# Feed-forward activations of a two-block transformer turned by VectorE and a trip through DRAM

## The chip, the core and the metric

One core of one Trainium2 chip runs the kernel. The metric is the device time of one launch in microseconds (us), the median of the timed runs. The engines are named as in the profile: PE is TensorE (PEld its weight loads), DVE is VectorE, ACT is ScalarE, POOL is GpSimd, SP is SyncE, which here only issues DMAs.

## What is computed

Two transformer blocks on a sequence of 256 tokens with 1024 features, all in f32. Cut to what matters, with the attention and mixing parts named only:

```python
# first block
h = rmsnorm(x, attn_norm_g);  qa, ka, va, qb, kb, vb = split(h @ w_in)
out_a = attention(rope(rmsnorm(qa)), rope(rmsnorm(ka)), va)      # 8 query heads, 2 key heads
out_b = differential_attention(rmsnorm(qb), rmsnorm(kb), vb, lam, rel_bias)
x = x + concat(out_a, out_b) @ w_out
u = square(relu(rmsnorm(x, mlp_norm_g) @ w_up))                  # 256 x 4096
x = x + u @ w_down
# second block; sh, sc, g come from silu(c) @ w_ada + b_ada
u = rms_norm(x, ffn1_norm_g) * (1 + sc1) + sh1
a, b = split(u @ ffn1_w_in);  x = x + 0.5 * g1 * ((silu(a) * b) @ ffn1_w_out)   # 256 x 2816
x = x + g2 * mixing(x)                                           # mLSTM, forgetting attention, gates
a, b = split(u3 @ ffn2_w_in); x = x + 0.5 * g3 * ((silu(a) * b) @ ffn2_w_out)   # 256 x 2816
```

## The kernel before, in words

Every product with weights is made of three TensorE matmuls on fp32r halves. A weight or activation W is split into an upper part hi (its value rounded to fp32r) and a lower part lo = W - hi, and A @ W is taken as Ahi@Whi + Ahi@Wlo + Alo@Whi (lines 1217, 1221 and 1222, in the function `half`). The moving operand is 512 columns of weights, the stationary one 128x128 of the activation, turned so that features lie on partitions. There are two tiles t of 128 tokens. So each 128x512 piece of weights costs 6 matmuls, 3 for each tile.

Weights come in units of two such pieces (128 x 1024 numbers, 512 KB). A unit goes through three steps. SP issues its DMA into one of four `raw` buffers, ACT writes `whi` (L1525), and DVE writes `wlo` (L1907). There are five pairs of `whi` and `wlo` (NW = 5), and three lent ones at the start of a stage. SP may issue the load of a unit when DVE is done with the unit four before it, and ACT may make `whi` when PE is done with the unit five before it.

The order of all work is made ahead by a planner (`plan`). It walks over the halves (a unit on one tile), and after each half it ticks a list of jobs. The table LAG says how many ticks a job waits between its steps, LO says how many halves DVE's `wlo` stands behind ACT's `whi` in each stage, and ADA says after how many halves a step of the modulation is made. Such a step multiplies 512 KB of w_ada (an `araw` buffer, line 2247) by silu(c) on DVE. Each engine then works through its own list strictly in order, and semaphores connect them. PACED names the blocks with several ticks for each half.

In a feed-forward stage PE makes a block of 512 hidden columns (`up0` to `up7`, or `a` and `b` of a gated one). For `up` ACT takes relu from PSUM into a buffer `nat` and DVE squares it (L2292). For a gated block DVE multiplies the two (L2302). The result has tokens on partitions and must be turned for the next product. The job has two steps (`turn_segments`), each with 4 TensorE transposes of 128x128 against `ident` (L1270, 256 hidden columns of both tiles) into a bank of PSUM. ACT copies the bank to the upper part (`uh`, L1627), and DVE writes the lower part from the bank and the upper part (`ul`, L1911). The first block has 8 hidden blocks of 512. Each of ffn1 and ffn2 has 5 of 512 and one of 256 columns. That makes 16 + 11 + 11 = 38 banks, so 152 transposes.

In the attention stage the blocks of w_in come in the order qb, kb, vb, qa, ka. A plain head (qa, ka) is normed and rotated by tables (rope, a chain of DVE operations, lines 2036 to 2098). qb and kb are only normed. The scores of the differential part start when qb and kb are there, and those of the plain part when qa and ka are.

Of the kernel before, what the change touches and what calls it, by code (L numbers as in the profile page):

```python
# [21 lines left out]
LAG = {("attn", "sums"): 5, ("attn_a", "wait"): 21, ("attn_as", "round"): 4, ("attn_as", "wait"): 0,  # L22
       ("attn_as", 0): 6, ("attn_as", 1): 4, ("attn_as", 2): 3, ("attn_as", 3): 12, ("attn_at", "round"): 8,
       ("attn_at", 0): 4, ("attn_at", 1): 5, ("attn_at", 2): 3, ("attn_at", 3): 3, ("attn_at", 4): 1,
       ("attn_at", 5): 10, ("attn_at", 6): 1, ("attn_at", 7): 17, ("attn_aw", "round"): 3, ("attn_aw", 0): 4,
       ("attn_aw", 1): 3, ("attn_aw", 2): 8, ("attn_aw", 3): 1, ("attn_aw", 4): 7, ("attn_aw", 5): 4,
       ("attn_aw", 6): 1, ("attn_aw", 7): 17, ("attn_b", "wait"): 2, ("attn_bm", "round"): 10, ("attn_bm", 0): 2,
       ("attn_bm", 1): 1, ("attn_bm", 2): 2, ("attn_bm", 3): 4, ("attn_bs", "round"): 4, ("attn_bs", "wait"): 0,
       ("attn_bs", 0): 4, ("attn_bs", 1): 4, ("attn_bs", 2): 4, ("attn_bs", 3): 4, ("attn_bt", "round"): 5,
       ("attn_bt", 0): 1, ("attn_bt", 1): 6, ("attn_bt", 2): 7, ("attn_bt", 3): 1, ("attn_bw", "round"): 16,  # L30
       ("attn_bw", 0): 2, ("attn_bw", 1): 2, ("attn_bw", 2): 3, ("attn_bw", 3): 1, ("conv", 0): 3, ("conv", 1): 3,
       ("conv", 2): 4, ("end", "late"): 3, ("end", "lead"): 4, ("ffn1", "between0"): 0, ("ffn1", "between1"): 0,
# [2783 lines left out]
```

## Time and profile before

| what | us |
|---|---|
| median of 3 timed runs | 980.27 (980.14 to 983.6) |
| the profiled execution, its own time | 980.24 |
| its span, first to last instruction | 978.9 |
| PE busy in it | 963.1 (98%) |
| DVE, ACT, POOL busy | 701.4, 523.0, 56.2 |

The span leaves out 1.3 us of the execution. A busy PE here is not PE at its peak, since each matmul's recorded duration overlaps the next one's. What a matmul takes from the path is the distance from its start to the next start. The share of a stage that an engine is busy is read from the view by stretches, and what ended an idle stretch from the view of waits.

### The profile page before, as it was taken

To read this page: it belongs to the slowest core of one execution; us is meant where nothing else is said; L and a number is where in the kernel's file an instruction comes from. 1 tells how busy PE (TensorE), PEld (TensorE's weight loads), DVE (VectorE), ACT (ScalarE), POOL (GpSimd) and SP (SyncE) were. 2 spreads that over 40 slices of the span, in tenths; PEclk is the share of its full clock that TensorE was granted. 3 is DMA by queue.
4 is the path that set the end of the run, shared out by engine and by line. 5 is a ranking of instruction groups with operands and counts; after the bars stand their busy time and mean duration, and the time that the engine had idled before them with its cause. 6 is when DMAs were issued, how large, how long until landed. Compare 5 with 4: busy or idle time off the path is not lost.

```text
span 978.9 us, 12466 instructions
## 1 busy us (share of the span) xinstructions
PE 963.1 (98%) x4614; PEld 792.9 (81%) x4614; DVE 701.4 (72%) x1045; ACT 523.0 (53%) x800; POOL 56.2 (6%) x62
## 2 busy tenths in 40 slices
PE   9988999999999999999999999999999999999998
PEld 7777888888888888888788888877888878888886
DVE  6787678987776676687669987578768764555553
ACT  7576665554446444443576565477554474444431
POOL 2311000000000000000000121121000000000000
PEclk9999999999999999999999999999999999999999
DMA  9641768887894888888747775865637535555561
GB/s 342 216 151 44 237 214 279 299 292 258 291 359 137 297 275 276 280 276 291 250 128 228 246 238 175 269 214 187 213 119 245 195 118 184 171 185 193 203 215 43
DMA packets 110122, 216.19 MB, mean 221 GB/s; under 512 B 8242, under 2 KB 15562, under 8 KB 109806
## 3 DMA queue, kind: packets, MB, share of 16 engines
q1 hardware_dynamic: 109918, 215.13, 65.5%
q8 instruction: 36, 0.59, 0.2%
q10 hardware_dynamic: 144, 0.27, 0.1%
q14 instruction: 24, 0.20, 0.1%
HBM read 214.29 MB, written 2.13 MB: 221 GB/s over the span
## 4 chain that ended last, share of the span: by engine, by line
PE 91%; DVE 3%; ACT 2%; DMA 2%; issue 1%; POOL 0%; SPq 0%; ACTq 0%; DVEq 0%; POOLq 0%
PE ps L1217 28%; PE ps L1222 27%; PE ps L1221 27%; PE ps L1270 3%; PE ps L1357 2%; PE ps L1312 1%; PE ps L1338 1%; DMA NF<-scr_g 1%; PE ps L1248 1%; ACT whi L1525 1%; DMA raw<-in_w_mix 1%; DVE wlo L1907 1%; DMA raw<-in_w_in 0%; DVE nat L1990 0%; DVE x L1994 0%
## 5 line engine op out<-in xcount | busy, mean ns | idle before, releaser
L1525 ACT ACTIVATE whi<-raw 128x1024 fp32r<-128x1024 f32 (+1 forms) x300 | 311.4, 1047 | 263.0 <-PE ps L1222 208.0
L1907 DVE TENSOR_TENSOR wlo<-raw,whi 128x1024 fp32r<-128x1024 f32 (+1 forms) x300 | 358.1, 1211 | 70.9 <-ACT whi L1525 70.3
L1217 PE MATMUL ps<-whi,hTh 128*128 128x512 f32 (+1 forms) x800 | 319.7, 400 | 1.1 <-ACT hTh L1537 1.1
L1221 PE MATMUL ps<-wlo,hTh 128*128 128x512 f32 (+1 forms) x800 | 311.1, 389 | 0.0
L1222 PE MATMUL ps<-whi,hTl 128*128 128x512 f32 (+1 forms) x800 | 311.0, 389 | 0.0
L1217 PEld LDWEIGHTS ps<-whi,hTh 128*128 128x128 f32 x800 | 150.8, 189 | 32.3 <-issue 2.2
L1222 PEld LDWEIGHTS ps<-whi,hTl 128*128 128x128 f32 x800 | 150.7, 188 | 32.0
L1221 PEld LDWEIGHTS ps<-wlo,hTh 128*128 128x128 f32 x800 | 150.9, 189 | 28.6 <-issue 0.4
L2502 POOL TENSOR_TENSOR stat<-stat,mhalf 128x8 f32<-128x8 f32 (+3 forms) x29 | 36.2, 1259 | 606.0 <-DVE stat L1923 485.8
L1217 PE MATMUL ps<-whi,uh_ffn 128*128 128x512 f32 x176 | 69.2, 393 | 0.0
L1222 PE MATMUL ps<-whi,ul_ffn 128*128 128x512 f32 x176 | 68.6, 390 | 0.0
L1221 PE MATMUL ps<-wlo,uh_ffn 128*128 128x512 f32 x176 | 68.6, 390 | 0.0
L1911 DVE TENSOR_TENSOR ul_ffn<-ps,uh_ffn 128x512 fp32r<-128x512 f32 x22 | 15.2, 691 | 70.5 <-ACT uh_ffn L1627 70.5
L2247 DVE CUSTOM_DVE_ANT_0 araw<-araw,crow,colp 128x1024 f32<-128x1024 f32 x48 | 61.3, 1278 | 0.8 <-DMA araw<-in_w_mod 0.6
L1217 PE MATMUL ps<-whi,uh 128*128 128x512 f32 x128 | 50.3, 393 | 0.0
L1222 PE MATMUL ps<-whi,ul 128*128 128x512 f32 x128 | 49.9, 390 | 0.0
L1221 PE MATMUL ps<-wlo,uh 128*128 128x512 f32 x128 | 49.9, 389 | 0.0
L1222 PEld LDWEIGHTS ps<-whi,ul_ffn 128*128 128x128 f32 x176 | 33.0, 188 | 7.0
L1221 PEld LDWEIGHTS ps<-wlo,uh_ffn 128*128 128x128 f32 x176 | 33.1, 188 | 6.7
L1217 PEld LDWEIGHTS ps<-whi,uh_ffn 128*128 128x128 f32 x176 | 33.1, 188 | 6.7
L2263 DVE SCALAR_TENSOR_TENSOR gate<-araw,cs,gate 128x512 f32<-128x512 f32 x42 | 32.4, 771 | 1.6 <-DMA araw<-in_w_ada 0.8
L1270 PE MATMUL ps<-ident,nat 128*128 128x128 f32 x208 | 31.1, 272 | 2.5 <-DVE nat L2089 1.4
(256 smaller groups left out, 1074.3 us busy)
## 6 DMA issues: line engine op xcount, KB each, us to landing
raw<-in_ffn_w_in SPq DMA_DIRECT2D x80, 512.0 KB, 4.6
raw<-in_w_mix SPq DMA_DIRECT2D x64, 512.0 KB, 4.5
araw<-in_w_mod SPq DMA_DIRECT2D x48, 512.0 KB, 5.3
raw<-in_ffn_w_out SPq DMA_DIRECT2D x44, 512.0 KB, 4.2
raw<-in_w_up SPq DMA_DIRECT2D x32, 512.0 KB, 5.2
raw<-in_w_down SPq DMA_DIRECT2D x32, 512.0 KB, 5.6
araw<-in_w_ada SPq DMA_DIRECT2D x24, 512.0 KB, 4.9
raw<-in_w_out SPq DMA_DIRECT2D x16, 512.0 KB, 3.8
```

The lines of the kernel that those rows point to most:

```text
L1217: pe.e.matmul(o, ah, h[:, j, :], start=s0, stop=False, skip_group_check=True)
L1221: pe.e.matmul(o, ah, l[:, j, :], start=False, stop=False, skip_group_check=True)
L1222: r = pe.e.matmul(o, al, h[:, j, :], start=False, stop=s1, skip_group_check=True)
L1248: r = pe.e.transpose(bank[:, c * 128:(c + 1) * 128], src[:, (4 * p + c) * 128:(4 * p + c + 1) * 128], ident[:, :])
L1270: r = pe.e.transpose(bank[:, c * 256 + t * 128:c * 256 + t * 128 + 128], src[t][:, (2 * p + c) * 128:(2 * p + c + 1) * 128], ident[:, :])
L1357: r = pe.e.matmul(ob[:, h * 64:(h + 1) * 64], buf[:, (nk * c + k) * 128:(nk * c + k + 1) * 128], (fV if a["fox"] else VA)[:, k, v0:v0 + 64 ...
L1525: act.e.activation(uflat(whi, u), uflat(raw, u), ACT.Copy).then_inc(hi.up(u), 1)
L1907: v.tensor_tensor(uflat(wlo, u), uflat(raw, u), uflat(whi, u).bitcast(f32), SUB).then_inc(lo_dve.up(u), 1)
L1911: v.tensor_tensor(o, bank, h.bitcast(f32), SUB).then_inc(lower.up(name, p), 1)
L2247: v.tensor_tensor_reduce(out=w, in0=w, in1=crow[:, :], scale=1.0, scalar=col("bada", 8 * m + i), op0=MUL, op1=ADD, accum_out=modc[:, 8 * m ...
L2263: r = v.scalar_tensor_tensor(acc, buf[:, k, :], cs[:, kt:kt + 1], acc, MUL, ADD)
L2502: g.tensor_tensor(o, a, mhalf[:, 0:n], ALU.pow).then_inc(rstd.up(*key), 1)
```

## The change

It has four parts.

1. The turned activation of each feed-forward block no longer goes over TensorE. DVE transposes the 128x512 `nat` tile in blocks of 32x32 into a `sq` buffer (`swaps`). SP stores that to DRAM (`scr_u`, 256 KB) and reads it back in another order of rows, as runs of 512 bytes, into one of four new landing buffers (`land_m`, `land_f`; `shuttle`). ACT copies it to `uh` (`uppers_of`) and GpSimd makes `ul` from both (`lowers_of`). The order of features that results is not the natural one, so the rows of w_down, ffn1_w_out and ffn2_w_out are permuted on the host, ahead of the launch.
2. qa is the first block of the attention stage, ahead of qb, kb, vb, ka.
3. PE's wait for an activation of these stages is now on GpSimd's lower part, for each tile.
4. All numbers of LAG, LO and ADA are new. ADA for the mlp stage goes from 3 to 4 and for y from 4 to 7, LO for mlp from 3 to 1, and for u_mlp from 3 to 0.

```diff
-       ("gates", 3): 11, ("gates", 4): 1, ("glu", "turn"): 5, ("glu", 0): 8, ("heads", "turn"): 5, ("heads", 0): 5,
+       ("gates", 3): 12, ("gates", 4): 2, ("glu", "fetch"): 3, ("glu", "upper"): 5, ("glu", "lower"): 4,
...
-PACED = ("kb", "vb", "qa", "ka", "ob0", "ob1", "gb0", "gb1")
-ADA = {"attn": 0, "ffn1": 4, "ffn2": 7, "merged": 8, "mix": 11, "mixT": 0, "mlp": 3, "u_ffn1": 4, "u_ffn2": 6,
-       "u_mlp": 3, "y": 4, "yb": 5}
-LO = {"attn": 3, "begin": 5, "ffn1": 3, "ffn2": 3, "merged": 0, "mix": 3, "mixT": 3, "mlp": 3, "u_ffn1": 1,
-      "u_ffn2": 0, "u_mlp": 3, "y": 2, "yb": 0}
+PACED = ("qb", "kb", "vb", "qa", "ka", "ob0", "ob1", "gb0", "gb1")
+ADA = {"attn": 0, "ffn1": 4, "ffn2": 8, "merged": 8, "mix": 11, "mixT": 0, "mlp": 4, "u_ffn1": 4, "u_ffn2": 5,
+       "u_mlp": 3, "y": 7, "yb": 5}
+LO = {"attn": 3, "begin": 2, "ffn1": 3, "ffn2": 0, "merged": 0, "mix": 3, "mixT": 3, "mlp": 1, "u_ffn1": 0,
+      "u_ffn2": 4, "u_mlp": 0, "y": 0, "yb": 2}
...
-    for key, c0, n in (("qb", 768, 512), ("kb", 1280, 512), ("vb", 1792, 512), ("qa", 0, 512), ("ka", 512, 256)):
-        block(key, "w_in", 0, 8, c0, n, "attn", small=6 * (key == "qb"))
+    for key, c0, n in (("qa", 0, 512), ("qb", 768, 512), ("kb", 1280, 512), ("vb", 1792, 512), ("ka", 512, 256)):
+        block(key, "w_in", 0, 8, c0, n, "attn", small=6 * (key == "qa"))
...
+        def shuttle(name, kind):
+            land = land_of(name)
+            for t in range(2):
+                while None not in sqr.held or None not in land.held:
+                    yield 1
+                sqr.take(name, t)
+                land.take(name, t)
+            seg(name)
+            natural_end(name)
...
+            yield lag(kind, "fetch", 3)
+            seg(name)
+            yield lag(kind, "upper", 3)
+            seg(name)
+            yield lag(kind, "lower", 1)
+            seg(name)
...
-            yield from turn_segments(name, 2, "u")
-            natural_end(name)
+            yield from shuttle(name, "u")
...
         if act[:2] == "u_":
-            return lower(f"{act[2:]}g{k // 4}", p)
+            return u_low(hidden(act, k), t)
...
+        def uppers_of(name, dst, c0, n):
+            for t in range(2):
+                act.wait_ge(*ld_u[land_of(name).at(name, t)](name, t))
+                act.e.activation(by_blocks(dst, c0, n, t), landed(name, t, n), ACT.Copy).then_inc(upper.up(name, t), 1)
...
+        def swaps(name, ready, n):
+            for t in range(2):
+                dve.wait_ge(*ready(name, t))
+                dve.wait_ge(*sqr.free(name, t))
+                v.transpose(sqr.buf(name, t)[:, 0:n], nat.buf(name, t)[:, 0:n]).then_inc(swapped.up(name, t), 1)
+                nat.give(swapped(name, t), name, t)
...
+        def lowers_of(name, h, l, c0, n):
...
+            for t in range(2):
+                pool.wait_ge(*upper(name, t))
+                g.tensor_tensor(by_blocks(l, c0, n, t), landed(name, t, n), by_blocks(h, c0, n, t).bitcast(f32),
+                                SUB).then_inc(u_low.up(name, t), 1)
+                land_of(name).give(u_low(name, t), name, t)
...
+            for t in range(2):
+                sp.wait_ge(*swapped(name, t))
+                sp.wait_ge(*land.free(name, t))
+                i = sqr.at(name, t)
+                q.dma_start(bass.AP(scrU.tensor, land.at(name, t) * 65536, [[n, 128], [1, n]]),
+                            sqr.buf(name, t)[:, 0:n]).then_inc(st_u[i].up(name, t), 16)
+                sqr.give(st_u[i](name, t), name, t)
+            yield
+            for t in range(2):
+                sp.wait_ge(*st_u[sqr.at(name, t)](name, t))
+                sp.wait_ge(*mm(*behind))
+                q.dma_start(land.buf(name, t)[:, 0:n].rearrange("p (a x) -> p a x", a=4),
+                            bass.AP(scrU.tensor, land.at(name, t) * 65536, [[n // 4, 128], [32 * n, 4], [1, n // 4]])).then_inc(
+                                ld_u[land.at(name, t)].up(name, t), 16)
```

DVE in the middle of the `up` stage, one block of 512 hidden columns. L2247 and L2288 are the modulation step, L2292 and L2340 the square. Before:

```order
208 L2292 TENSOR_TENSOR nat<-nat 128x512 x2
209 L1911 TENSOR_TENSOR ul<-ps,uh 128x512
210 L1907 TENSOR_TENSOR wlo<-raw,whi 128x1024
211 L2247 ISA araw,modc<-araw,crow,colp 128x1024
212 L2247 ISA modc 128x1
213 L1911 TENSOR_TENSOR ul<-ps,uh 128x512
214 L1907 TENSOR_TENSOR wlo<-raw,whi 128x1024
215 L2247 ISA araw,modc<-araw,crow,colp 128x1024
216 L2247 ISA modc 128x1
217 L1907 TENSOR_TENSOR wlo<-raw,whi 128x1024 x2
```

And now:

```order
214 L2340 TENSOR_TENSOR nat<-nat 128x512 x2
215 L1948 TENSOR_TENSOR wlo<-raw,whi 128x1024
216 L2288 ISA araw,modc<-araw,crow,colp 128x1024
217 L2288 ISA modc 128x1
218 L1948 TENSOR_TENSOR wlo<-raw,whi 128x1024
219 L2333 STREAM_TRANSPOSE sq<-nat 128x512 x2
220 L1948 TENSOR_TENSOR wlo<-raw,whi 128x1024
221 L2288 ISA araw,modc<-araw,crow,colp 128x1024
222 L2288 ISA modc 128x1
223 L1948 TENSOR_TENSOR wlo<-raw,whi 128x1024
```

Two transposes of SBUF stand where two lower parts from PSUM stood, and a block has 2 modulation steps where it had 2 or 3.

SP in the same stage; `araw` is a modulation load. Before:

```order
40 L2611 DMA raw<-in_w_up 128x2x512 x2
41 L2654 DMA araw<-in_w_mod 128x1024
42 L2611 DMA raw<-in_w_up 128x2x512
43 L2654 DMA araw<-in_w_mod 128x1024
44 L2611 DMA raw<-in_w_up 128x2x512 x2
```

And now, one block:

```order
47 L2682 DMA raw<-in_w_up 128x2x512
48 L2705 DMA scr_u<-sq 128x512 x2
49 L2682 DMA raw<-in_w_up 128x2x512
50 L2745 DMA araw<-in_w_mod 128x1024
51 L2712 DMA land_m<-scr_u 128x4x128 x2
52 L2682 DMA raw<-in_w_up 128x2x512 x2
53 L2745 DMA araw<-in_w_mod 128x1024
```

Two stores, each behind a wait for DVE's transpose, and two loads, each behind a wait for its store, stand among 4 weight loads and 2 modulation loads.

PE at the end of block ka, from its last weight matmul on. `kd` holds the rotated keys, VB and PT belong to the differential part, `over` and PA to its softmax. Before:

```order
252 L1222 MATMUL ps<-whi,hTl 128x256
253 L1270 MATMUL ps<-ident,nat 128x128 x4
254 L1372 MATMUL ps<-VB,PT 128x128 x4
255 L1338 MATMUL ps<-ident,over 128x128 x4
256 L1270 MATMUL ps<-ident,nat 128x128 x4
257 L1372 MATMUL ps<-VB,PT 128x128 x8
258 L1270 MATMUL ps<-ident,kd 128x128 x4
259 L1312 MATMUL ps<-kaT,qaT 128x256 x8
260 L1338 MATMUL ps<-ident,P 128x128 x8
```

And now:

```order
250 L1266 MATMUL ps<-whi,hTl 128x256
251 L1356 MATMUL ps<-kbT,qbT 128x256 x4
252 L1382 MATMUL ps<-ident,PA 128x128 x4
253 L1416 MATMUL ps<-VB,PT 128x128 x4
254 L1382 MATMUL ps<-ident,over 128x128 x4
255 L1416 MATMUL ps<-VB,PT 128x128 x4
256 L1314 MATMUL ps<-ident,kd 128x128 x4
257 L1382 MATMUL ps<-ident,over 128x128 x4
258 L1356 MATMUL ps<-kaT,qaT 128x256 x8
259 L1416 MATMUL ps<-VB,PT 128x128 x4
```

The transposes of the queries are gone from here, one group of four scores of the differential part has come in, and 8 of the products with VB now stand behind the plain scores.

## Rows read from the trace of the kernel before

**Rows 1.** The page, busy time and instructions of each engine:
```profile
PE 963.1 (98%) x4614; PEld 792.9 (81%) x4614; DVE 701.4 (72%) x1045; ACT 523.0 (53%) x800; POOL 56.2 (6%) x62
```
**Rows 2.** The page, chain that ended last, shares of the span by engine:
```profile
PE 91%; DVE 3%; ACT 2%; DMA 2%; issue 1%; POOL 0%; SPq 0%; ACTq 0%; DVEq 0%; POOLq 0%
```
**Rows 3.** PE's waits: who it waited for, us in total, times, longest:
```profile
PE ps L1270 <- DVE nat L2089: 1.4, 1, 1.4
...
PE ps L1270 <- DVE kd L2098: 1.2, 1, 1.2
```
**Rows 4.** Time line of PE: start us, us, engine, line, operation:
```profile
143.30 0.39 PE L1217 MATMUL ps<-whi,hTh 128*128 128x512 f32 x1
...
143.76 0.39 PE L1222 MATMUL ps<-whi,hTl 128*128 128x512 f32 x1
143.99 0.60 PE L1270 MATMUL ps<-ident,nat 128*128 128x128 f32 x4
144.34 0.48 PE L1217 MATMUL ps<-whi,hTh 128*128 128x512 f32 x1
144.66 0.40 PE L1221 MATMUL ps<-wlo,hTh 128*128 128x512 f32 x1
```
**Rows 5.** Time line of DVE in the up stage:
```profile
194.44 0.68 DVE L1911 TENSOR_TENSOR ul<-ps,uh 128x512 fp32r<-128x512 f32 x1
195.04 1.21 DVE L1907 TENSOR_TENSOR wlo<-raw,whi 128x1024 fp32r<-128x1024 f32 x1
196.17 1.27 DVE L2247 CUSTOM_DVE_ANT_0 araw<-araw,crow,colp 128x1024 f32<-128x1024 f32 x1
197.38 0.08 DVE L2247 DVE_READ_ACCUMULATOR2_ANT modc<- 128x1 f32 x1
```
**Rows 6.** Stretches: us, PE, PEld, DVE, ACT, POOL busy, PEclk, DMA share, GB/s:
```profile
190.00:201.00 11.00, 11.00 (x54) 9.12 (x53) 10.27 (x14) 6.37 (x8) 0.00 (x0) 1.00 0.91 308
...
267.00:278.00 11.00, 11.00 (x50) 9.13 (x49) 8.70 (x11) 4.25 (x4) 0.00 (x0) 1.00 1.01 390
...
396.00:418.00 22.00, 22.00 (x102) 18.21 (x101) 15.74 (x19) 10.56 (x12) 0.00 (x0) 1.00 0.85 283
```
**Rows 7.** DVE groups, shapes apart: busy us, mean ns:
```profile
L2292 DVE TENSOR_TENSOR nat<-nat 128x512 f32<-128x512 f32 x16 | 10.9, 689 | 6.3 <-ACT nat L1756 6.2
...
L1947 DVE CAST hTh<-sq 128x512 fp32r<-128x512 f32 x8 | 3.4, 424 | 2.1 <-ACT sq L1563 1.9
```
**Rows 8.** Time line of POOL and DVE in the mixing stage:
```profile
643.57 2.53 POOL L2538 TENSOR_TENSOR nat<-nat,row 128x512 f32<-128x512 f32 x2 [5.13 <-ACT nat L1839]
...
644.92 2.27 DVE L1907 TENSOR_TENSOR wlo<-raw,whi 128x1024 fp32r<-128x1024 f32 x1 [2.60 <-ACT whi L1525]
```
**Rows 9.** Time line of ACT and PE, one weight unit (whi at 187.50, PE at 199.30):
```profile
187.50 1.06 ACT L1525 ACTIVATE whi<-raw 128x1024 fp32r<-128x1024 f32 x1 [1.66 <-PE ps L1222]
...
199.30 0.39 PE L1221 MATMUL ps<-wlo,hTh 128*128 128x512 f32 x1
```
**Rows 10.** DMA issues: queue, operation, KB each, median us to landing:
```profile
raw<-in_w_up SPq DMA_DIRECT2D x32, 512.0 KB, 5.2
...
biasT<-scr_b SPq DMA_DIRECT2D x8, 128.0 KB, 2.5
out<-x SPq DMA_DIRECT2D x4, 256.0 KB, 2.2
```
**Rows 11.** SP's waits, the longest on a store: us in total, times, longest:
```profile
SPq L2639 <- DMA scr_b<-scr_t: 5.1, 1, 5.1
```
**Rows 12.** Time line of PE and DVE at the end of block ka:
```profile
67.96 0.28 PE L1222 MATMUL ps<-whi,hTl 128*128 128x256 f32 x1
...
77.74 3.16 PE L1312 MATMUL ps<-kaT,qaT 64*128 64x256 f32 x16 [0.78 <-ACT kaT L1605]
...
72.57 0.27 DVE L2036 TENSOR_REDUCE stat<-sq 128x2 f32<-128x128 f32 x1
...
75.35 0.89 DVE L2098 TENSOR_TENSOR kd<-nat,stat 128x128 f32<-128x128 f32 x4
```

More of the change, by code:

```diff
@@ L19 @@
 NEVER = (None, 0)
[L22 to L32, printed above, removed]
@@ L263, in build @@
     sX.close()
+    sY = ExitStack()
+    sb("under_mlp", [128, 16384], c=sY)
+    land_m = Ring([sb(f"land_m{i}", [128, 512], c=sY) for i in range(4)])
+    sY.close()
+    sZ = ExitStack()
+    sb("under_ffn", [128, 14336], c=sZ)
+    land_f = Ring([sb(f"land_f{i}", [128, 512], c=sZ) for i in range(4)])
+    sZ.close()
     whi += [lent_hi[j] for j in range(LENT)]
@@ L282, in build, with land_of @@
     scrG = nc.dram_tensor("scr_g", (24, 256), f32, kind="Internal").ap()
+    scrU = nc.dram_tensor("scr_u", (4, 128, 512), f32, kind="Internal").ap()
+    def land_of(name):
+        return land_m if name[:2] == "up" else land_f
     columns = {}
@@ L495, in half @@
             at["act"] = blocks[units[u][0]]["act"]
+            if at["act"][:2] == "u_":
+                drain_of([hidden(at["act"], k) for k in range(units[u][2], units[u][2] + units[u][3])])
             for w in lows:
@@ L798, in plan @@
         at["ada"] = ada()
[L799 removed]
+        pairs.take("qa")
         for k in range(8):
@@ L807, in plan @@
             order.append(("first_lo", k))
-        first = blocks["qb"]["units"]
+        first = blocks["qa"]["units"]
         for u in first:
@@ L868, in job_glu @@
             yield lag("glu", 0, 3)
-            yield from turn_segments(name, (n + 255) // 256, "glu")
-            natural_end(name)
+            yield from shuttle(name, "glu")
         def ffn(m, last_gate, stage, then=None):
@@ L2293, in up_job @@
             yield
-            yield from lowers(name, 2, uh["mlp"], ul["mlp"], 4 * c)
+            swaps(name, squared, 512)
+            yield
+            yield
+            yield
         def glu_job(m, i, n):
@@ L2304, in glu_job @@
             yield
-            yield from lowers(name, n // 256, uh[m], ul[m], 4 * i)
+            swaps(name, glu, n)
+            yield
+            yield
+            yield
         def gates_job():
@@ L2625, in row, with shuttle @@
                 load_row(d["b_mix"], at + c * 512, name)
+        def shuttle(name, n, behind):
+            land = land_of(name)
+            yield
+            for t in range(2):
+                sp.wait_ge(*swapped(name, t))
[4 more added lines that the diff above has]
+                sqr.give(st_u[i](name, t), name, t)
+            yield
+            for t in range(2):
+                sp.wait_ge(*st_u[sqr.at(name, t)](name, t))
[3 more added lines that the diff above has]
+                                ld_u[land.at(name, t)].up(name, t), 16)
+            yield
+            yield
         def bias_job():
@@ L2712, in sync_program @@
         jobs = {"bias": bias_job(), "ada": ada(), "gates": gates_job()}
+        for c in range(8):
+            jobs[f"up{c}"] = shuttle(f"up{c}", 512, (blocks["up0"]["units"][LENT - 1], 1))
+        for m, last in (("ffn1", "down1"), ("ffn2", "wob1")):
+            for i in range(6):
+                jobs[f"{m}g{i}"] = shuttle(f"{m}g{i}", 512 if i < 5 else 256, last_half(last))
         for what, *of in order:
@@ L2804, with shuttled @@
     w_mod = np.stack([np.asarray(inputs["w_ada_2"])[0, :, m * D:(m + 1) * D].T for m in (0, 1, 3, 4, 6, 7)])
+    def shuttled(name):
+        w, n = data[name][0], data[name].shape[1]
+        full = w[:n // 512 * 512].reshape(-1, 4, 4, 32, w.shape[1]).transpose(0, 2, 3, 1, 4).reshape(-1, w.shape[1])
+        rest = w[n // 512 * 512:].reshape(-1, 4, n % 512 // 128, 32, w.shape[1]).transpose(0, 2, 3, 1, 4) if n % 512 else w[:0]
+        return np.ascontiguousarray(np.concatenate([full, rest.reshape(-1, w.shape[1])])[None])
+    data.update({name: shuttled(name) for name in ("w_down", "ffn1_w_out", "ffn2_w_out")})
     data.update(w_mod=np.ascontiguousarray(w_mod), colp=np.ascontiguousarray(colp), w_gate=w_gate,
```

89 lines of the change are left out of this document (57 added, 32 removed), and 25 rows, old and new, of the table LAG.

## The prediction, made before the changed kernel was run

> **What bounds the kernel now.** I read the page first. PE is busy 98% of the span [rows 1], and the chain that ended last lies on PE for 91% of it, with DVE, ACT and DMA at 2 or 3% each [rows 2]. So the kernel is bound by the number and pitch of TensorE instructions. PE's waits, read next, are short and few. The long ones of the attention stage are 1.4 and 1.2 us [rows 3], and in the time line of starts I count 6.4 us of such gaps between 67.9 and 82 us. In the up stage and the gated ones PE waits for nothing: it is busy 11.00 of 11.00 us in each stretch [rows 6].
>
> Whatever leaves PE's list in those stages therefore shortens the run by its whole pitch, as long as the other engines keep up. The stretches say which could fail to. In the up stage DVE is busy 10.27 of 11 us and the DMA engines have a share of 0.91 [rows 6]. In the gated stage DVE has 15.74 of 22 and DMA 0.85.
>
> **What a group of four transposes costs.** Weight matmuls start 0.23 us apart: two of them take 143.30 to 143.76 [rows 4]. Around a group the start of the matmul ahead is 143.76 and the second start behind it 144.66, which is 0.90. Two pitches of that are 0.45, so a group of four costs 0.45. It is more than the 0.35 from 143.99 to 144.34, since the first matmul behind it takes 0.32 and not 0.23. There are 38 such groups, all in stages where PE never waits, and the other 37 have the same spacing within 0.02. **Term 1: 38 x 0.45 = -17.1 us.**
>
> **What takes their place.** For each hidden block (8 in the first stage, 6 in each gated one, 20 in all) and each tile there are now a DVE transpose, a store, a load, an ACT copy and a GpSimd subtraction, so 40 of each (4 of them half as wide). PE sees them only if an activation or a weight is late.
>
> *The activations themselves.* up7 ends before down0 starts and is read by its last eighth, 28 halves of 1.37 us = 38 us later. Its steps are 5 + 1 + 15 + 2 ticks, at one tick a half, 31 us, and the order holds the last within it. The last gated block needs 1 + 3 + 5 + 4 ticks and is read at the last two of 22 halves. Cost 0, hidden behind the product with the blocks ahead. If a trip took 7 us longer than its ticks, this cover would be gone and the excess would be paid once in each of three stages.
>
> *ACT.* 40 copies replace 38 from PSUM of the same size. ACT is busy 6.4 of 11 us, so cost 0.
>
> *DVE.* The transpose is not in the trace. Its bounds are a 128x512 cast at 0.42 us and a 128x512 product at 0.69 us [rows 7]. I take 0.69 less the overlap, 0.61, the start-to-start of the lower part that it replaces (194.44 to 195.04 [rows 5]), because that row is limited to one element at a time as well. The Trainium skill, "Vector Engine (DVE) Microarchitecture Reference", § 3.8, says the 32x32 transpose sustains one element per cycle per lane, so a row of a tile would take what the product takes; no run here shows it, and the sum would be the same.
>
> One block of the up stage takes PE 48 x 0.227 = 10.9 us. DVE has in it, by starts: 4 wlo x 1.13 (195.04 to 196.17), 2 modulation steps x 1.21, 2 squares x 0.69 and 2 transposes x 0.61 [rows 5, 7] = 9.5 us, against 10.3 before. That alone is a little relief.
>
> *GpSimd against DVE.* The 128x512 product of GpSimd takes 1.3 us (two in 2.53), and while the second of them ran, from about 644.8 to 646.1, DVE's wlo of 644.92 took 2.27 us and not 1.21 [rows 8, 5]. So a GpSimd operation that reads two SBUF tiles holds back a DVE operation that does. The Trainium skill, "SBUF — State Buffer", § Who interferes with whom, states this as an exclusive lock on a port pair, held for a whole instruction, between GpSimd reads and a DVE instruction with two SBUF inputs; by that rule, the trace agrees, with 1.06 us lost in one meeting. Nearly all DVE work of a block (wlo, modulation, square) is of that kind. Two subtractions a block cost DVE between 0 (they fall beside a transpose or an idle moment) and 2 x 1.3 = 2.6 us, and I take 2.2 since DVE is seldom idle. DVE then needs 9.5 + 2.2 = 11.7, in the worst case 12.1, of 10.9 us. Over 8 blocks it falls 6 to 10 us behind. The strided 32-element runs that GpSimd now reads are not in the trace. I take the contiguous price and keep a dearer one for a rival.
>
> *DMA.* A block moves 4 weights and 2 modulation loads of 0.524 MB and 4 shuttle transfers of 0.262 MB: 4.19 MB in 10.9 us is 385 GB/s, against 308 at a share of 0.91 before. The highest stretch before is 390 GB/s at a share of 1.01, and 308 at 0.91 would give 338 at a full share [rows 6]. So the engines are full: a block takes 10.7 to 12.4 us of them, a lag of 0 to 1.5 a block over about 7 blocks, 0 to 10 us. I take the row of 390, since a saturated queue is the state ahead, so under 1 us in all.
>
> *The slack.* A unit's whi starts at 187.50, as PE lets go of the buffer, its wlo ends at 194.5 and PE reads it at 199.30 [rows 9, 5]: 4.8 us to spare. LO for this stage goes from 3 to 1 halves, which gives up to 2 x 1.37 = 2.7 more, so 7.5. DVE's and DMA's lags run side by side and draw on the same slack. DVE's 6 to 10 less 7.5 leaves 0 to 3. **Term 2: +3 us** in the up stage and the start of down, with ends 0 (the lags stay inside the slack) and 12 (10 of DMA and 10 of DVE in part one after the other, less 7.5).
>
> *SP.* Its list is in order, so a store waits for DVE's transpose and a load for its store, and weight loads queue behind both. A store of 256 KB lands in 2.2 us, and the one wait on a store through DRAM was 5.1 us [rows 10, 11]. One weight and one modulation load stand between store and load in the up stage, so SP is held some 2 to 4 us once a block. The weight behind it is late by as much, inside the same 7.5 us. The load itself resembles the 128 KB read of biasT from DRAM (2.5 us) up to the 5.2 of a weight.
>
> *The gated stages.* A block of 512 columns takes PE 21.8 us. DVE had 15.74 of 22, and 2.6 more fit. DMA goes from 283 GB/s to 283 + 48 = 331 [rows 6], inside 338 to 390. **Term 3: +0.5 us**, ends 0 and 3.
>
> **Attention.** The plain queries' rotation now comes in the first blocks, where PE has other weights. Before, PE ended ka at 67.96 and began the plain scores at 77.74, 9.8 us later. DVE did two weights and the rest of the queries' rotation first. The keys' chain began at 72.57 and ended with kd at 76.24, 3.7 us [rows 12]. Now DVE has four masked softmax steps of about 0.5 us ahead of it, which wait for scores about 0.6 us behind the block's end. So kd is there after 0.6 + 2.0 + 3.7 = 6.3 us. What is late next is the last pair of softmax parts (1.3 us more), whose transposes stand ahead of the plain scores. They start about 8.0 us after the block and not 9.8, with about as many PE instructions in between. 8 products with VB now fill the wait for the first exponentials. The differential part has less weight work to hide behind (vb and ka, not vb, qa and ka), which can bring new gaps of a like size. **Term 4: -1.5 us**, ends -3.5 and +4.
>
> **The other numbers** of LAG move steps in the mixing stage, where no PE work is added or removed and PE's gaps sum to under 6 us. I take 0, ends -2 and +2.
>
> **The sum.** 978.9 - 17.1 + 3 + 0.5 - 1.5 = 963.8 us of span. The execution is 1.3 longer: 965.1. The profiled execution (980.24) and the median (980.27) are the same, so nothing is corrected. Predicted: 965 us, a ratio of 0.984.
>
> **Rivals.**
> 1. *The up stage runs at DVE's or the DMA engines' pace.* For it: DVE's 11.7 to 12.1 of 10.9 us and 385 GB/s asked for. Against it: 7.5 us of slack, and less load as soon as `down` begins. Term 2 is then 8 to 12, so 970 to 974.
> 2. *GpSimd's strided subtraction is dear, and the run is slower than before.* For it: no row has its pattern, and DVE is held for as long as it runs. Against it: the contiguous row of 1.3 us. With a price p, a block needs 9.5 + 2p of DVE, and 8 blocks lose 8 x (9.5 + 2p - 10.9) - 7.5. From p = 2.5 the loss exceeds the 18 us gained; at 3.3 it is 34 us, and 965 - 3 + 34 = 996. It decides in the up stage, where PE would wait on wlo.
> 3. *The lags stay inside the slack and attention closes its gaps.* Term 2 is 0 and term 4 is -3.5: 978.9 - 17.1 - 3.5 + 1.3 = 959.6, say 960 to 962.
> 4. *The gain is given back in pieces*, late activations after each stage, SP held behind stores, and new gaps in attention: +6, +3 and +4 on top of term 2, so about 977.
>
> **Chances.** The forecast (962 to 969) 0.53, rival 3 0.12, rival 1 0.2, rival 4 0.08, rival 2 0.07. A measurement of this kernel can tell about 0.5% (4.9 us) from no change. Faster by more than that means below 975.4: 0.53 + 0.12 + 0.2 + a little of rival 4 = 0.87. Within it: 0.06. Slower: 0.07. The range from 960 to 976 holds the first three and leaves out rival 2, most of rival 4 and the edge of rival 3.
>
> **What would show it.** Term 1: 152 fewer transposes, and PE's starts around the `up` blocks 0.23 us apart throughout. Term 2: in the stretches of the up stage PE's busy time stays near 11.00 of 11, DVE's goes above 10.3, wlo operations of over 2 us appear beside GpSimd's, and the DMA share is near 1. If PE's waits name wlo or whi there for more than 8 us, rival 1 holds. GpSimd's subtraction at about 1.3 us clears rival 2, and above 2.5 it proves it. Term 4: the plain scores begin about 8 us after ka's last matmul. The prediction is wrong if GpSimd's price, the landing of the 512-byte runs (above 7 us) or a clock that falls in the new gaps is other than taken here.

## The result and the profile after

| | changed kernel | before, on the same chip |
|---|---|---|
| median of 5 runs, us | 974.52 (971.50 to 975.37) | 983.41 (980.14 to 986.04) |
| ratio | 0.9915, 95% interval 0.9894 to 0.9937 | 1 |
| profiled span, us | 974.0 | 978.9 |

The change makes the kernel 0.85% faster, where 1.6% was forecast. The time lies in the range and the direction is right, but half of the gain is missing. A few executions, among them one of e6 and one of e7 below, ran at a much lower granted clock (1350 to 1816 us) and are left out of all ratios. The page of the changed kernel, busy time by engine (it answers to [rows 1]) and the chain that ended last by engine ([rows 2]):

```profile
PE 949.5 (97%) x4462; PEld 780.3 (80%) x4462; DVE 719.1 (74%) x1047; ACT 524.6 (54%) x803; POOL 124.9 (13%) x102
```
```profile
PE 80%; DMA 8%; DVE 6%; ACT 3%; issue 2%; POOL 1%; SPq 0%; DVEq 0%; ACTq 0%; POOLq 0%
```

The 152 transposes are gone and PE's busy time fell by 13.6 us, but the span only by 4.9. The chain was on PE for 91% and is now for 80%, with DMA at 8%. To see where, I noted the start of PE's first weight matmul of each stage. The table has the lengths of the stages in the profiled runs, in us. The first stage begins with PE's first weight matmul, 6 us into the span, the last ends with the span, and e2, e7 and e10 come below:

| stage | before | changed | e2 | e7 | e10 |
|---|---|---|---|---|---|
| start to up | 113.7 | 113.0 | 113.0 | 115.1 | 112.5 |
| up | 93.8 | 88.0 | 88.0 | 88.1 | 88.0 |
| down | 91.1 | 102.3 | 90.1 | 90.2 | 94.0 |
| ffn1, both products | 188.4 | 182.5 | 181.7 | 181.8 | 182.3 |
| mixing | 293.1 | 294.2 | 293.7 | 293.5 | 297.4 |
| ffn2, both products | 192.6 | 187.7 | 187.7 | 187.7 | 187.1 |

The up stage gained all that its 12 groups were to give. What is missing was lost in down, which has 4 groups fewer and still takes 11.2 us more. Stretches of the changed kernel, the view of [rows 6], with the same columns. The first one spans the end of up (down starts at 207.3 us), the others lie in down:

```profile
201.00:212.00 11.00, 11.00 (x50) 9.13 (x49) 10.03 (x11) 6.17 (x8) 3.14 (x2) 1.00 1.02 365
212.00:223.00 11.00, 10.81 (x48) 8.63 (x47) 8.17 (x10) 6.32 (x8) 3.51 (x2) 1.00 1.01 339
223.00:234.00 11.00, 10.12 (x42) 7.35 (x40) 10.35 (x10) 5.28 (x6) 3.28 (x3) 1.00 0.93 329
234.00:245.00 11.00, 8.79 (x36) 6.60 (x36) 7.37 (x9) 3.18 (x3) 0.00 (x0) 1.00 1.00 349
245.00:256.00 11.00, 6.03 (x16) 4.78 (x17) 9.26 (x9) 4.63 (x7) 3.17 (x2) 0.69 0.96 324
256.00:267.00 11.00, 11.00 (x50) 9.10 (x49) 7.69 (x10) 5.55 (x9) 0.00 (x0) 1.00 0.79 250
```

DVE is not busy throughout, so it isn't what is late. Its waits and ACT's between 200 and 250 us show who is: `wlo` waits for `whi`, and `whi` for the loads of w_down. The gate row of the modulation (L1450) then waits for DVE, once and long:

```profile
ACT whi L1555 <- DMA raw<-in_w_down: 23.9, 14, 6.8
DVE wlo L1948 <- ACT whi L1555: 7.4, 4, 3.3
...
PE ps L1450 <- DVE gate_lo L2310: 5.4, 1, 5.4
...
PE ps L1261 <- DVE wlo L1948: 2.9, 5, 1.3
```

PE's time line there, and the clock behind it in stretches of 4 us:

```profile
244.18 0.39 PE L1266 MATMUL ps<-whi,ul 128*128 128x512 f32 x1
249.97 0.77 PE L1450 MATMUL ps<-row_hi,ones 128*128 128x512 f32 x1 [5.40 <-DVE gate_lo L2310]
...
250.97 0.63 PE L1261 MATMUL ps<-whi,uh 128*128 128x512 f32 x1
251.39 0.63 PE L1265 MATMUL ps<-wlo,uh 128*128 128x512 f32 x1
```
```profile
248.00:252.00 4.00, 2.03 (x5) 1.68 (x6) 4.00 (x3) 2.24 (x3) 2.96 (x2) 0.56 0.99 274
252.00:256.00 4.00, 4.00 (x13) 3.10 (x12) 2.30 (x4) 0.01 (x1) 0.00 (x0) 0.59 0.88 334
256.00:260.00 4.00, 4.00 (x19) 3.31 (x18) 2.53 (x4) 2.11 (x2) 0.00 (x0) 1.00 0.55 165
```

By starts (what the distance to the next start exceeds the usual 0.227 us by), PE's waits in down add up to 10.5 us, 5.6 of them before the gate row; in e2, which has the same list, 1.0. The granted clock is at its half level (1.2 GHz) from 248.5 to 255.3 us. PE stands idle for the first 1.5 us of that, and from 249.97 on 12 starts follow each other at 0.43 us and more, not 0.23, which costs 2.6 more. Together 9.5 + 2.6 = 12.1 us, of the 12.2 that down takes beyond that of e2 (90.1, where 91.1 - 1.8 = 89.3 would be without the 4 groups): nearly the whole loss.

**Why the loads are late.** The weights' lead over PE (from the end of a unit's `wlo` to PE's first use of it) drains for the most part before down, in up: it is 8.0 to 8.5 us in the middle of up, 1.7 at its end and 0.4 in down. From 150 to 215 us the DMA view of the changed kernel shows (first the GB/s in 40 slices of 1.6 us, then the issues: queue, operation, KB each, median us from issue to landing):

```profile
GB/s 315 268 391 418 391 340 366 269 306 338 412 378 210 253 222 303 353 377 403 421 300 297 320 308 266 359 413 413 287 259 297 333 334 401 408 401 320 346 368 261
DMA packets 13899, 21.82 MB, mean 336 GB/s; under 512 B 826, under 2 KB 5946, under 8 KB 13895
...
raw<-in_w_up SPq DMA_DIRECT2D x14, 512.0 KB, 7.5
...
scr_u<-sq SPq DMA_DIRECT2D x10, 256.0 KB, 9.0
```

The time line of SP's issues, one and a half blocks (L2705 stores, L2712 reads back):

```profile
175.48 0.33 SPq L2745 DMA_DIRECT2D araw<-in_w_mod  x1
181.78 1.02 SPq L2712 DMA_DIRECT2D land_m<-scr_u  x2
182.84 1.02 SPq L2682 DMA_DIRECT2D raw<-in_w_up  x2
183.90 0.47 SPq L2745 DMA_DIRECT2D araw<-in_w_mod  x1
184.41 0.47 SPq L2682 DMA_DIRECT2D raw<-in_w_up  x1
185.08 2.66 SPq L2705 DMA_DIRECT2D scr_u<-sq  x2
187.79 0.68 SPq L2682 DMA_DIRECT2D raw<-in_w_up  x1
188.53 0.56 SPq L2745 DMA_DIRECT2D araw<-in_w_mod  x1
194.33 1.05 SPq L2712 DMA_DIRECT2D land_m<-scr_u  x2
```

SP issues nothing between 175.8 and 181.8 and between 189.1 and 194.3, since the next item in its list must wait for the store, which takes 9 us to land behind the loads already queued. Afterwards SP issues the overdue loads in one burst, behind which the next store waits again. The rate stays high during most of a hold (353 to 421 GB/s in the slices from 176 to 182 us) and falls behind it: 300 to 266 from 182 to 191 us, 287 and 259 from 195.5, and 210 to 253 from 169.5, behind a hold that ended at 169.1. The queue never runs empty, though. By issue and landing at least 3 transfers (1.3 MB) are under way at each microsecond from 150 to 232. So the time line ties the lower rate to the holds, but doesn't show what inside the DMA engines lowers it. The share of 0.99 in this window also fits another reading, that the engines can give no more than 336 GB/s with this mix of runs. So there were four theories:

- **A**: the DMA engines are at their limit, some 340 GB/s.
- **B**: SP, held by the wait for the store, issues weight loads too late.
- **C**: GpSimd's subtractions hold DVE, and DVE is late.
- **D**: the new numbers (LO, the modulation's pace) cost the time, not the trip.

### The profile page after: what moved, and what is told of

It is laid out like the page before. It is cut to its first block, busy times and chain, and to the rows that moved or that the text cites. A ratio compares the mean times of both kernels' runs of the same rounds, so it can differ in the third digit from the quotient of the medians.

```text
span 974.0 us, 12407 instructions
## 1 busy us (share of the span) xinstructions
PE 949.5 (97%) x4462; PEld 780.3 (80%) x4462; DVE 719.1 (74%) x1047; ACT 524.6 (54%) x803; POOL 124.9 (13%) x102
## 4 chain that ended last, share of the span: by engine, by line
PE 80%; DMA 8%; DVE 6%; ACT 3%; issue 2%; POOL 1%; SPq 0%; DVEq 0%; ACTq 0%; POOLq 0%
PE ps L1261 24%; PE ps L1266 24%; PE ps L1265 24%; DMA raw<-in_w_up 3%; DVE wlo L1948 2%; DMA araw<-in_w_ada 2%; PE ps L1401 2%; PE ps L1314 1%; ACT whi L1555 1%; PE ps L1356 1%; DMA raw<-in_w_down 1%; PE ps L1382 1%; DMA NF<-scr_g 1%; DMA scr_u<-sq 1%; PE ps L1292 1%
## 5 line engine op out<-in xcount | busy, mean ns | idle before, releaser
L1948 DVE TENSOR_TENSOR wlo<-raw,whi 128x1024 fp32r<-128x1024 f32 (+1 forms) x300 | 369.2, 1245 | 128.1 <-ACT whi L1555 127.1
L2646 POOL TENSOR_TENSOR ul_ffn<-land_f,uh_ffn 128x512 fp32r<-128x512 f32 (+1 forms) x24 | 40.4, 1703 | 229.5 <-ACT uh_ffn L1798 229.5
L2288 DVE CUSTOM_DVE_ANT_0 araw<-araw,crow,colp 128x1024 f32<-128x1024 f32 x48 | 64.4, 1341 | 0.0
L2646 POOL TENSOR_TENSOR ul<-land_m,uh 128x512 fp32r<-128x512 f32 x16 | 27.0, 1707 | 100.2 <-ACT uh L1798 100.2
```

The costliest lines, as they stand in the source:

```text
L1948: v.tensor_tensor(uflat(wlo, u), uflat(raw, u), uflat(whi, u).bitcast(f32), SUB).then_inc(lo_dve.up(u), 1)
L2288: v.tensor_tensor_reduce(out=w, in0=w, in1=crow[:, :], scale=1.0, scalar=col("bada", 8 * m + i), op0=MUL, op1=ADD, accum_out=modc[:, 8 * m ...
L2646: g.tensor_tensor(by_blocks(l, c0, n, t), landed(name, t, n), by_blocks(h, c0, n, t).bitcast(f32), SUB).then_inc(u_low.up(name, t), 1)
```

## The experiments

Each ratio is to the kernel before on the same chip, from four to six runs.

| run | ratio (95%) | span, us | down, us |
|---|---|---|---|
| e1 thin modulation loads | 0.9779 (0.9757 to 0.9800) | 959.8 | 89.2 |
| e2 fetch after 4 ticks | 0.9786 (0.9762 to 0.9810) | 960.5 | 90.1 |
| e3 up by TensorE | 0.9866 (0.9844 to 0.9887) | 969.8 | 91.9 |
| e4 modulation slower in down | 0.9835 (0.9809 to 0.9862) | 967.7 | 97.9 |
| e5 read back by GpSimd's queue | 0.9801 (0.9782 to 0.9820) | 959.3 | 89.5 |
| e6 fetch after 2 ticks | 0.9916 (0.9888 to 0.9944) | 966.9 | 96.7 |
| e7 e2 with old attention | 0.9837 (0.9814 to 0.9861) | 962.3 | 90.2 |
| e8 e2, lower parts by DVE | 0.9815 (0.9795 to 0.9834) | 962.4 | 90.0 |
| e9 changed kernel again | 0.9914 (0.9890 to 0.9938) | 973.4 | 102.9 |
| e10 e2 with old pace and LO | 0.9851 (0.9833 to 0.9869) | 967.5 | 94.0 |
| e11 fetch after 8 ticks | 0.9794 (0.9774 to 0.9814) | 960.0 | 89.7 |

### Bytes or waits: e1 and e2

e1 cuts the bytes (the modulation loads of up and down bring 32 KB each and not 512, so its modulation isn't the model's):

```diff
+                if 2 <= n < 32:
+                    dst, src = araw.buf(n)[:, 0, 0:64], d["w_mod"][0, 0:128, 0:64]
                 q.dma_start(dst, src).then_inc(ld_ada[araw.at(n)].up(n), 16)
```

> Loads 2 to 31 of the modulation (those of the up and the down stage) move 32 KB and not 524 KB; all waits, the order and DVE's work on the buffers stay. The modulation computed is therefore a wrong one, so the time tells only what the bytes cost. Theory A (the DMA engines are full in the up stage and in the first third of down, at about 340 GB/s where 385 are asked for): the demand falls to about 300 GB/s in up and 200 in down, weights are never late, the down stage takes about 89 us and not 102.4, the whole about 962 us (ratio to the kernel before 0.979). Theory B (SP's in-order list, which waits 37 us for the completion of stores between 150 and 250 us, makes the weight loads late): the waits stand where they stood, at most 3 us gained, 971 to 974. Theory C (GpSimd's subtraction holds DVE and DVE is what is late): no change, 974.

e2 keeps them and moves the wait:

```diff
-       ... ("u", "fetch"): 1, ("u", "upper"): 15,
+       ... ("u", "fetch"): 4, ("u", "upper"): 12,
```

> In the up stage SP reads a block back 4 ticks after its store and not 1, and ACT's copy comes 12 ticks after that and not 15, so bytes and activation times are the same but 3 ticks (4 us) of weight loads now stand between store and load. Theory B (SP's wait for the store is what delays the weights): SP's waits for stores fall from 37 us to under 10, and 5 to 8 us are gained, 967 to 970. Theory A (the DMA engines' capacity): the same bytes in the same stage, 973 to 975.5, no difference. Theory C: no change.

e1 took 961.3 us, as A said, and e2 961.8, better than B said. Alone, e1 would have shown the wrong cause. B was wrong to expect that the waits stay when the bytes go: a store behind shorter queues lands sooner, and SP's waits for stores (150 to 250 us) fell from 37.4 us to 11.4. e2 decides, since it moves the same bytes. The same DMA view, 150 to 215 us, of e2:

```profile
GB/s 275 347 410 417 373 329 383 367 398 421 406 370 384 412 408 403 401 399 366 403 393 401 377 396 381 366 383 386 371 381 371 374 379 417 405 384 406 397 358 402
DMA packets 16289, 25.02 MB, mean 385 GB/s; under 512 B 953, under 2 KB 7097, under 8 KB 16285
...
raw<-in_w_up SPq DMA_DIRECT2D x14, 512.0 KB, 6.3
...
scr_u<-sq SPq DMA_DIRECT2D x10, 256.0 KB, 5.6
```

The deep dips are gone (the rate stays above 325 after the first slice), the mean is 385 and not 336 GB/s, and a store lands in 5.6 us. The stretch from 150 to 215 us by engine, of the changed kernel and then of e2, with the share of the DMA engines and the rate at its end:

```profile
150.00:215.00 65.00, 65.00 (x288) 53.86 (x287) 54.46 (x64) 33.38 (x42) 17.05 (x10) 1.00 0.99 336
```
```profile
150.00:215.00 65.00, 65.00 (x289) 53.81 (x288) 61.03 (x71) 39.35 (x48) 19.11 (x12) 1.00 1.05 385
```

The waits of SP's queue in that window, of the changed kernel and then of e2, show what took their place, the wait for DVE to free a buffer, which the table of `raw` buffers makes in any case:

```profile
SPq L2712 <- DMA scr_u<-sq: 26.8, 10, 6.0
...
SPq L2682 <- DVE wlo L1948: 2.7, 6, 0.7
```
```profile
SPq L2682 <- DVE wlo L1948: 17.1, 21, 1.8
...
SPq L2712 <- DMA scr_u<-sq: 8.3, 12, 2.1
```

PE waits for nothing between 112 and 270 us, and the slow clock in down is gone with the gap ahead of it. A falls. B's 5 to 8 us was too small, because it counted late weights alone and neither the gate row nor the clock behind it.

### The same wait on another engine: e5

In the blocks of the up stage SP's list has neither the wait nor the load, and GpSimd's has both at the same step:

```diff
+                    pool.wait_ge(*st_u[sqr.at(name, t)](name, t))
+                    pool.wait_ge(*mm(blocks["up0"]["units"][LENT - 1], 1))
+                    g.dma_start(land.buf(name, t)[:, 0:512]...
```

> As the changed kernel, with its fetch lag of 1 and all its numbers, but the 16 loads that bring a block of the up stage back are issued by GpSimd's queue, and GpSimd waits there for the store, not SP. The bytes, the issue order of all other loads and the moment from which a block may be read back stay. Theory B (SP, held in its in-order list by the wait for a store, issues the weight loads late and the DMA queues run empty): with the wait gone from SP's list the gain of the late fetch comes fully, 960 to 963 us, and the stretches of the up stage show about 385 GB/s. Theory A (the DMA engines give no more than some 340 GB/s with this mix of short and long runs): 973 to 976.

961.3 us, and the mean from 150 to 215 us is 381 GB/s. The fetch is as early as in the changed kernel and no lag moved. But one thing more differs. The DMA view of e5 for 150 to 215 us has hardly a packet of 512 bytes:

```profile
DMA packets 10814, 24.76 MB, mean 381 GB/s; under 512 B 940, under 2 KB 940, under 8 KB 10810
```

Issued by GpSimd, the read-back went in packets of 4096 bytes and not of 512, so e5 alone could also speak for a dear read in short runs. e2 excludes that, since it keeps these packets (7097 under 2 KB) and reaches 385 GB/s. Taken together, the wait's place in SP's list is the cause, and not the read itself. The Trainium skill, "DMA: Bandwidth & Descriptors", § Issuing engines are not separate DMA queues, says that issuing from several engines saves only the issuing sequencer's time, usually small beside the transfer. That it saves nothing more agrees with these runs, as e2, with one issuing engine, reaches the same rate (385). What the sequencer lost here was not small, as it held a wait.

### The dose: e6 and e11

The diff is that of e2, with 2 and 14, and with 8 and 8.

> A dose between the changed kernel (fetch after 1 tick, 974.5) and e2_late_fetch (4 ticks, 961.8): 2 ticks of 1.37 us, ACT's copy one tick less behind it. Theory B: the hold for each store falls by about 1.4 us from 5.7 to some 4, and as the backlog in the queue sets the rest, the gain is partly there: 964 to 970, with SP's waits for stores between 150 and 250 us at 20 to 30 us in sum. Had the late fetch helped by some other effect of the shifted steps (a threshold at the copy's time), 2 ticks would read as 1, 974, or as 4, 962, with SP's wait not in proportion.

> The changed kernel with the fetch after 8 ticks and the copy 8 ticks behind it (1 and 15 there, 4 and 12 in e2). Theory B says that all is gained once the store has landed before SP comes to it: SP's waits for stores go from 9.9 us in sum to 0 and there is nothing left to gain, 960.5 to 962. If SP's list mattered through the place of the load and not through the wait, 8 would go on from 4, below 959, or turn back.

e11 took 962.1 us with no wait for a store at all in SP's list between 150 and 250 us: four ticks were enough, as B says. e6 missed its mark. Its waits for stores came to 30.5 us there (37.4 in the changed kernel), and its ratio is that of the changed kernel. Its runs spread from 968.3 to 975.4, and the profiled one is the fastest, so its 96.7 us of down flatter it. The gain doesn't follow the dose, and 2 ticks read as 1, which the expectation had given to the other theory, a threshold somewhere in the shifted steps. e5 speaks against that, as it moved no step and gained all. A likely reason is that a tick (1.37 us) counts only once SP comes so late that no burst builds up, whose loads make the next store late; that wasn't tried by itself.

### The numbers or the trip: e3, e4, e10

e3 sends up0 to up7 over TensorE again (turn, copy and lower part as in the kernel before, rows of w_down in natural order):

```diff
+            if int(name[2]) in BY_PE:
+                yield 10
+                yield from turn_segments(name, 2, "u")
+                natural_end(name)
+                return
             yield lag("u", 0, 4)
             yield from shuttle(name, "u")
```

> Only the up stage goes back to TensorE's transposes: its 8 blocks have 16 groups of 4 transposes, ACT and DVE make the parts from PSUM, and the rows of w_down are in natural order. The gated stages and every number of the tables stay as in the changed kernel. The transposes cost 16 x 0.45 = 7.2 us. Theory A: the demand in up falls from 385 to about 290 GB/s and the 13 us lost in down and its slow clock come back: 974.5 + 7.2 - 13 = 969. Theory D (the 13 us come from the new table numbers, LO 1 and 0 and the modulation's pace, and not from the trip through DRAM): 974.5 + 7.2 = 982.

969.5 us: up back at 93.8, down at 91.9, as theory A had forecast. B, which then has no store to wait for, says the same. D falls. In the up stage the trip as built was a loss of 5 us, and all of the change's gain came from the gated stages. With the late fetch it gains 8 there.

e4 changes two numbers of ADA:

```diff
-ADA = {"attn": 0, "ffn1": 4, ...
+ADA = {"attn": 0, "ffn1": 3, ...
...
-       "u_mlp": 3, "y": 7, "yb": 5}
+       "u_mlp": 4, "y": 7, "yb": 5}
```

> The modulation's pace in the down stage is one step each 4 halves and not 3, and in ffn1 3 and not 4, so 4 of its loads (2.1 MB) move from down to ffn1. Theory A: the demand in down falls from 319 to 287 GB/s, against 340 that the engines give, so the weights catch up after some 25 us and not 45, and the gate row at 244 us no longer holds PE for 5.4 us: 4 to 7 us gained, 0 to 2 lost in ffn1, 969 to 972. Theory B or C: within 1 us of 974.5.

967.4 us, a little more than A had forecast, while B had expected no change and was wrong there. Down takes 97.9 and ffn1 loses nothing. But PE waits already between 212 and 223 us (9.29 us busy of 11), as SP's waits for stores stay (41.1 us). It cures what follows from the lost lead and not its cause.

e10 is e2 with one number of ADA (mlp) and two of LO (mlp and u_mlp) changed:

```diff
-ADA = {... "mixT": 0, "mlp": 4, ...
+ADA = {... "mixT": 0, "mlp": 3, ...
...
-LO = {... "mixT": 3, "mlp": 1, ... "u_mlp": 0, ...
+LO = {... "mixT": 3, "mlp": 3, ... "u_mlp": 3, ...
```

> e2_late_fetch with the modulation's pace in up at one step each 3 halves (as before the change) and not 4, and LO for up and down at 3 and 3 and not 1 and 0. Per block of the up stage (10.9 us) 2.67 modulation loads come and not 2: 4.54 MB, 416 GB/s asked, where e2 showed 382 to 395 at a share of 1.04 to 1.06. If that is the engines' limit, each block lags by 10.9 x (416 - 390) / 390 = 0.7 us, some 5 us over 7 blocks, and LO takes away 2 to 4 us of the lead of 6.0 that e2 kept; so the lead falls to between -1 and 1 us, PE waits for up to 3 us, and with a slow clock behind it the time is 962 to 967. If the numbers of the tables are worth nothing, 961.8 within 1 us. If they were what made the trip through DRAM affordable (the prediction took 2.7 us of slack from LO), it is 967 or more.

967.4 us, just past the upper end. So with the late fetch the new numbers are worth some 5 us (962.1 for e11 on the same chip), LO and the pace together. Asked for 416 GB/s the engines gave 386 from 150 to 215 us, and the least lead in down fell from 6.0 us in e2 to 0.4, as in the changed kernel. That doesn't show 386 to be the engines' limit, for DVE had more to do as well and was busy 43.18 of 44 us:

```profile
157.00:201.00 44.00, 44.00 (x196) 36.41 (x195) 43.18 (x52) 23.91 (x30) 15.48 (x8) 1.00 1.04 381
```

Which of the two drained the lead stays open. Down took 94.0. The mixing stage lost 3.7 more, which the expectation didn't have. Of that, 1.6 lie in its stretch from 669.6 to 698.4 us, where the granted clock was at half from 669.8 to 673.2 us, which it isn't in e2. Its modulation steps fall at other places, and which of them cost the rest wasn't tried.

### DVE, GpSimd and attention: e7, e8, e9

> The changed kernel as it is, beside the next two on one chip, so that they can be compared with it directly: 974.5 us, a ratio of 0.9915 to the kernel before.

It was 973.8 us, 0.9914, and its down stage was 102.9 with the same 5.4 us before the gate row.

e8 makes the lower parts in DVE's list, at the same step:

```diff
-                g.tensor_tensor(by_blocks(l, c0, n, t), landed(name, t, n), ...
+                v.tensor_tensor(by_blocks(l, c0, n, t), landed(name, t, n), ...
```

> e2_late_fetch with the 40 lower parts made by VectorE in the same step and not by GpSimd. Theory C in its weak form (GpSimd's reads hold DVE, about 1.3 us an operation, so moving them to DVE costs DVE no more): DVE's busy time of 42.4 us between 157 and 201 stays within 1.5 us of that, since 8 subtractions of about 0.7 come and as much stretching of other operations goes; PE waits for neither, 961.8 within 1 us. If DVE had paid nothing for GpSimd's work, its busy time there rises by 5 to 6 us to 48 of 44, the lead of the weights drains, and the time is 966 to 972.

963.0 us (e5 on the same chip: 961.3). One stretch of e2 and then of e8:

```profile
157.00:201.00 44.00, 44.00 (x196) 36.44 (x195) 42.41 (x51) 26.71 (x34) 12.82 (x8) 1.00 1.04 386
```
```profile
157.00:201.00 44.00, 44.00 (x196) 36.41 (x195) 42.78 (x58) 26.51 (x33) 0.00 (x0) 1.00 1.05 386
```

The subtraction itself, e2 on GpSimd and e8 on DVE (ns, least, median, most):

```profile
L2646 POOL TENSOR_TENSOR ul<-land_m,uh x14: 1286/1883/2387, 157.5 to 225.1; 128x512 fp32r<-128x512 f32 x14
```
```profile
L2339 DVE TENSOR_TENSOR ul<-land_m,uh x14: 682/684/689, 160.8 to 230.2; 128x512 fp32r<-128x512 f32 x14
```

DVE does 8 x 0.684 = 5.5 us more work there and is busy only 0.4 us longer. Where the rest went is seen in the group of `wlo` in the same stretch, e2 and then e8 (busy us, mean ns):

```profile
L1948 DVE TENSOR_TENSOR wlo<-raw,whi 128x1024 fp32r<-128x1024 f32 x17 | 24.4, 1435 | 1.6 <-ACT whi L1555 1.0
```
```profile
L1948 DVE TENSOR_TENSOR wlo<-raw,whi 128x1024 fp32r<-128x1024 f32 x17 | 20.6, 1213 | 1.2 <-ACT whi L1555 1.2
```

In e2 its 17 `wlo` had been stretched by 3.8 us, 0.47 for each of the 8 GpSimd subtractions, and its other operations took the same in both. (The remaining 1.3 us isn't stretching: among other things the stretch holds 9 modulation operations in e2 and 8 in e8.) The Trainium skill, "SBUF — State Buffer", § Who interferes with whom, describes an exclusive lock on a port pair that does this to a DVE instruction with two SBUF inputs. The trace agrees, in both directions, since GpSimd's 1.29 us become 1.88 in the median. C falls in its strong form, as PE didn't wait for DVE in e2 either way.

e7 is e2 with the blocks of attention in the old order and the old numbers up to `up`.

> e2_late_fetch with the attention stage as in the kernel before: blocks in the order qb, kb, vb, qa, ka and the old numbers for every step up to the up stage (the list of work up to there is word for word that of before), the rest as in e2. The stages as read from the traces say that the new order gained 0.7 us up to the up stage, so 961.8 + 0.7 = 962.5 (962 to 963.5). The prediction's term 4 said 1.5 us: 963.3. Should the slow stretches of TensorE's clock (6.8 us in the new attention, 3.4 in the old) outweigh the gaps closed, it is 960 to 961.5.

Against e5 on the same chip it is 0.36% or 3.5 us slower, more than the stages of two profiles had said, and at the good end of term 4. In the profiles of e7 and e5 the stages up to `up` took 115.1 and 113.3 us. But the new attention took 115.6 in e8 and the old one 113.7 in the kernel before, and the intervals of e5 and e7 overlap by a little, so the direction is likely and the size is not settled. The clock mixes in: in the new attention it is at half for 6.8 us (71.0 to 77.8 in the changed kernel), in the kernel before for 3.4 us and in e7's profile not at all.

## The prediction, step by step

**Term 1 held** (-17.1 forecast). With the late fetch, where no lag disturbs it, up and down together are 6.8 us shorter (16 groups, 7.2), ffn1 6.7 and ffn2 4.9 (11 groups, 4.95 each): 18.4.

**Term 2 was mis-sized: +3 forecast, +12.2 measured** (102.3 against e2's 90.1, with the same transposes and the same DMA bytes). Of its steps:

- The DMA engines: to go by the row of 390 GB/s was right as far as it was needed. They gave the 385 that the stage asks for (e2), and 386 in e10.
- DVE: 11.7 us a block were forecast. In e2, 42.4 of 44 us are 10.5 in 10.9. The transpose took 0.686 us, as the product does, and the hold by GpSimd was 0.47 and not 1.1 us an operation.
- GpSimd: its strided subtraction costs 1.29 us where nothing holds it, as the contiguous row said. Rival 2 is excluded.
- **SP is the step that failed.** "A store of 256 KB lands in 2.2 us", so "SP is held some 2 to 4 us once a block", "inside the same 7.5 us". The 2.2 us were those of stores at the end of the run, with no weight loads around them. Here 9.0 us were measured, and SP waited 26.8 us in 65, 4.5 a block (the one row of such a wait had shown 5.1 us [rows 11], and I took 2 to 4). More important, I booked the hold as one delay inside a slack. It came again in every block of a stage that asks for 385 GB/s, and what it cost wasn't made up between two holds: the mean rate is 336 and not 385, by which the weights would fall behind by 10.9 x 49 / 336 = 1.6 us a block, and 11 over seven blocks (an estimate). All but 1.7 us of the lead is spent before down begins. How a hold lowers the rate while 3 or more transfers are still under way stays open.

My bound for the engines at 338 GB/s (a lag of up to 1.5 us a block) then happens to describe the rate that came about, for another reason. So the time lies at rival 1's upper end, 974, but DVE (busy 54.5 of 65 us) doesn't set the pace, and the DMA engines don't either. That the total fell inside the range is luck as far as this term goes.

**The slow clock** was named among the things that would make the prediction wrong, and had no price. It cost 2.6 us of the 12.2 in down.

**Term 3** (+0.5, ends 0 and 3): 0. The gated stages are 10.8 us shorter for 9.9 of transposes.

**Term 4** (-1.5, ends -3.5 and +4): -0.7 by the stages, about -3.5 by e7. The working was wrong in part. The keys' chain came no sooner. PE's last matmul of ka starts at about 65.5 us, kd is begun at 73.3 and the plain scores at 76.55, 11 us later, where 8 were forecast and 9.8 taken before [rows 12], with the other part's scores among them. PE's time line of the changed kernel shows what ended the waits ahead of them, softmax sums and parts, named as the next to be late:

```profile
69.97 0.66 PE L1382 MATMUL ps<-ident,over 128*128 128x128 f32 x4 [1.69 <-DVE stat L2168]
72.55 2.07 PE L1416 MATMUL ps<-VB,PT 128*128 128x128 f32 x8 [1.93 <-ACT PT L1739]
```

**The mixing stage** (0, ends -2 and +2): +1.0. (Rival 4's pieces add up to 978 and not 977, which changes nothing.)

**The sum by what was measured** (by unrounded starts, and with the first matmul 0.1 us later): 978.9 + 0.1 - 0.7 - 5.8 + 11.2 - 5.9 + 1.0 - 4.9 = 973.9, against 974.0.

The version with the late fetch (e2, e11) or with the read issued by GpSimd (e5) beats both kernels: 961.3 to 962.1 us, 2.0 to 2.1% below the kernel before and 12 us below the changed one. The late fetch costs two numbers of a table.

## What to carry to other kernels

A wait in the list of the engine that issues the DMAs stops all loads behind it. Price it by the landing time under the load of its own stage, and in a stage that asks for nearly all that the engines were seen to give count it as bandwidth lost in every round, not as one delay. Put enough other issues between a store and its read-back, or give the read-back to an engine whose list can afford the wait. When less traffic helps, check with an experiment that keeps the bytes and moves the wait before you say that bandwidth is the limit.
